# Entries and exits of two block-product feed-forwards, reordered

## What is computed

```python
    x = x + gt2[:, None, :] * ((jax.nn.silu(gate) * up) @ w_down[l])
    return rmsnorm(x, g_final)                 # of first_block
    ...
    h = h + 0.5 * swiglu(rms_norm(h, ffn1_norm[l]), ffn1_w_gate[l], ffn1_w_up[l], ffn1_w_down[l])
    u = rms_norm(h, mix_norm[l])
    z = u @ w_in[l]
    ...
    h = h + merged @ w_out[l]
    h = h + 0.5 * swiglu(rms_norm(h, ffn2_norm[l]), ffn2_w_gate[l], ffn2_w_up[l], ffn2_w_down[l])
    return rms_norm(h, final_norm)
```

## Time and profile before

| | |
|---|---|
| median of the runs | 1738.32 us |
| the profiled execution | 1740.45 us |
| its span, first to last instruction | 1738.6 us |
| mean granted TensorE clock | 0.987 |
| PE matmul busy | 1673.1 us, 96% |
| PE weight load busy | 1424.8 us, 82% |
| DVE busy | 1054.4 us, 61% |
| ACT busy | 735.4 us, 42% |
| POOL busy | 200.5 us, 12% |

### The profile page before, as it was taken

The page is one execution under the profiler, slowest core; times in us unless marked ns, Lnnn a source line. Parts: engine busy times, 40 slices in busy tenths (PEclk is TensorE's granted clock), DMA queues, the critical chain, the costliest instruction groups (busy, mean ns, idle before and its releaser), DMA issues.

```text
span 1738.6 us, 24842 instructions
## 1 busy us (share of the span) xinstructions
PE 1673.1 (96%) x9717; PEld 1424.8 (82%) x9717; DVE 1054.4 (61%) x1586; ACT 735.4 (42%) x1238; POOL 200.5 (12%) x193
## 2 busy tenths in 40 slices
PE   7999999999999978999999989999999899999998
PEld 5777688888888768989899877677887699898997
DVE  4888765433333475776767634766455677586774
ACT  3466544212222444524345322555443554243444
POOL 0120120000000262010010230002001210101102
PEclk9999999999999988999999999999999999999999
DMA  9733145342242537474575136212236474537721
GB/s 331 249 111 123 42 146 175 109 127 76 88 125 69 137 98 186 100 203 119 150 169 146 37 110 113 73 50 70 85 97 169 113 191 138 146 84 202 170 85 49
DMA packets 289159, 219.98 MB, mean 127 GB/s; under 512 B 15995, under 2 KB 275511, under 8 KB 289031
## 3 DMA queue, kind: packets, MB, share of 16 engines
q1 hardware_dynamic: 261056, 181.43, 33.7%
q0 software_dynamic: 27632, 36.89, 11.8%
q10 hardware_dynamic: 360, 0.13, 0.0%
HBM read 215.27 MB, written 6.36 MB: 127 GB/s over the span
## 4 chain that ended last, share of the span: by engine, by line
PE 40%; DVE 10%; ACT 5%; issue 5%; DVEq 0%; ACTq 0%
PE psum L695 9%; PE psum L697 9%; PE psum L696 9%; PE psum L1038 4%; PE psum L1041 3%; PE psum L1040 3%; DVE ring_lo L2179 3%; ACT ring_hi L1626 3%; PE psum L1182 1%; DVE part_raw L2187 1%; PE psum L1147 1%; PE psum L1202 1%; DVE c L2294 1%; DVE g_part L2276 1%; DVE sq L2268 1%
## 5 line engine op out<-in xcount | busy, mean ns | idle before, releaser
L2179 DVE TENSOR_TENSOR ring_lo<-part_raw,ring_hi 128x1024 fp32r<-128x1024 f32 (+1 forms) x270 | 324.7, 1203 | 233.4 <-ACT ring_hi L1626 232.8
L1626 ACT ACTIVATE ring_hi<-part_raw 128x1024 fp32r<-128x1024 f32 (+1 forms) x270 | 277.8, 1035 | 346.9 <-PE psum L697 270.7
L1038 PE MATMUL psum<-hq_hi,ring_hi 128*128 128x256 f32 x1232 | 354.2, 287 | 21.2 <-DVE hq_lo L2370 10.9
L1040 PE MATMUL psum<-hq_lo,ring_hi 128*128 128x256 f32 x1232 | 351.3, 285 | 0.0
L1041 PE MATMUL psum<-hq_hi,ring_lo 128*128 128x256 f32 x1232 | 351.1, 285 | 0.0
L1038 PEld LDWEIGHTS psum<-hq_hi,ring_hi 128*128 128x128 f32 x1232 | 239.2, 194 | 25.7 <-DVE hq_lo L2370 11.5
L1040 PEld LDWEIGHTS psum<-hq_lo,ring_hi 128*128 128x128 f32 x1232 | 239.3, 194 | 0.2
L1041 PEld LDWEIGHTS psum<-hq_hi,ring_lo 128*128 128x128 f32 x1232 | 239.1, 194 | 0.0
L695 PE MATMUL psum<-hid_hi,ring_hi 128*128 128x512 f32 (+1 forms) x536 | 208.5, 389 | 8.7 <-DVE hid_lo L2307 5.2
L697 PE MATMUL psum<-hid_hi,ring_lo 128*128 128x512 f32 (+1 forms) x536 | 207.7, 387 | 0.0
L696 PE MATMUL psum<-hid_lo,ring_hi 128*128 128x512 f32 (+1 forms) x536 | 207.5, 387 | 0.0
(11 more groups left out here) (300 smaller groups left out, 2514.5 us busy)
## 6 DMA issues: line engine op xcount, KB each, us to landing
part_raw<-in_ffn_w_up SPq DMA_DIRECT2D x66, 512.0 KB, 4.9
w_raw<-in_w_in SPq DMA_DIRECT2D x50, 512.0 KB, 3.7
part_raw<-in_w_gate_up SPq DMA_DIRECT2D x44, 512.0 KB, 4.5
part_raw<-in_ffn_w_gate SPq DMA_DIRECT2D x44, 512.0 KB, 5.6
part_raw<-in_ffn_w_down SPq DMA_DIRECT2D x32, 512.0 KB, 4.3
part_raw<-in_ffn_w_gate POOLq DMA_DIRECT2D x22, 512.0 KB, 8.2
part_raw<-in_ffn_w_up POOLq DMA_DIRECT2D x22, 512.0 KB, 10.3
sq<-in_w_ada SPq DMA_DIRECT2D x20, 512.0 KB, 4.8
```

What stands on the lines that cost most here:

```text
L1038: pe.matmul(o, a_hi, b_hi, start=fresh, stop=False, skip_group_check=True)
L1040: pe.matmul(o, a_hi, b_lo, start=False, stop=False, skip_group_check=True)
L1626: act.activation(ring_hi[slot][:, 0:n], pool_raw[s_][b][:, 0:n], ACT.Identity).then_inc(f_high, 1)
L2179: dve.tensor_tensor(ring_lo[slot][:, 0:n], raw_[:, 0:n], ring_hi[slot][:, 0:n].bitcast(F32), ALU.subtract).then_inc(f_ready, 1)
```

## The change

It has these parts.
- The squares of down0 and out2 are no longer added by POOL: `gather` issues, per tile, a DMA that accumulates sq into acc, and waits for its landing before it issues the next. ACT, TensorE and the first and third running copies wait for these landings (`gathered`).
- h is made in three groups per k: A11 and R3; N1 and R2; A12, A22 and N4. N1 and N4 are the negatives of R1 and R4, and signs are turned in the copies and in c12 and c22 to match. DVE makes N1 from x itself, before the second `take_h`, and the item's low part goes between.
- In unit 0 the token sums stand after the second half of B21 and the spreads after T4; the DVE and ACT parts of them move accordingly. B21 waits for all twelve groups.
- In every unit DVE does `first_up` before the item after T1. In the last unit of a round the hidden tiles are formed before the item after B22, and both silus stand after T4.
- The first two slabs of the projection after ffn1 are split before its last down product.
- out2 splits the first three weight items of ffn2 at steps 3, 4 and 6 and the fourth after step 7.
- The near_rows DMAs are issued before `add_weights(1, 0)`.
- In ffn0 the modulation rows are added one unit earlier, and their columns made before the last two hidden tiles enter the first two down products.

```diff
+AHEAD = [3, 4, 6]
...
-        A11, R3, A12, A22, R1, R2, R4 = range(7)
+        A11, R3, N1, R2, A12, A22, N4 = range(7)
...
             def token_sums(name, phase, kinds=1):
 
-                pe.wait_ge(summed, SUM0 + SQUARES[phase] + KD * kinds)
+                if phase in GATHERED:
+                    pe.wait_ge(gathered, 16 * (GATHERED[phase] + KD))
+                else:
+                    pe.wait_ge(summed, SUM0 + SUMMED[phase] + KD * kinds)
...
                 down_part(f, r, order[0], ks[:-2], True)
                 down_part(f, r, order[1], ks[:-2])
+                if between is not None:
+                    between()
                 down_part(f, r, order[0], ks[-2:], True)
                 down_part(f, r, order[1], ks[-2:])
-                if between is not None:
-                    between()
...
-                product(z, "T1", R1, f, u, first=True, ready=None if q0 is None else q0 + 2).then_inc(f_prod, 1)
-                if u == 0:
-                    sums()
+                product(z, "T1", N1, f, u, first=True, ready=None if q0 is None else q0 + 2).then_inc(f_prod, 1)
                 await_item(("T2", f, u))
-                pe.wait_ge(s1_set, m)
+                pe.wait_ge(run_copied, 3 * m - 2)
                 product(y, "T2", R2, f, u).then_inc(f_prod, 1)
                 await_item(("B21", f, u))
+                if u == 0:
+                    pe.wait_ge(q_ready, q0 + 3 * KQ)
...
                 product(x_, "B21", A12, f, u, (1,)).then_inc(f_prod, 1)
                 if u == 0:
+                    sums()
+                await_item(("T4", f, u))
+                pe.wait_ge(run_copied, 3 * m)
+                product(y, "T4", A22, f, u).then_inc(f_prod, 1)
+                if u == 0:
                     spreads()
-                await_item(("T4", f, u))
-                pe.wait_ge(u3_set, m)
-                product(y, "T4", A22, f, u).then_inc(f_prod, 1)
...
                 if u == 0:
-                    act.wait_ge(summed, SUM0 + SQUARES["down0" if f == 1 else "out2"] + KD * (2 if f == 1 else 1))
-                act.activation(s1, psum[:, y, :], ACT.Copy).then_inc(s1_set, 1)
+                    act.wait_ge(gathered, 16 * (KD * f - 1))
+                act.activation(s1, psum[:, y, :], ACT.Copy).then_inc(run_copied, 1)
...
-                wait_summed("down0", i, None, 2)
                 wait_new("down0", i, None, 1)
-                take_h(i, n, "ffn1", gff[:, n:n + 1])
+                take_h(n, "ffn1", gff[:, n:n + 1])
+                if n >= KQ:
+                    parts_high(n % KQ, 1, "ffn1")
+                if i >= 2:
+                    act.wait_ge(gathered, 16 * (i - 1))
                 for m in range(2):
                     act.activation(sq[:, i % 2, m, :], x[:, n, :], ACT.Square,
                                    scale=col_of("g_final", n, None, 1) if m else 1.0).then_inc(squared, 1)
-                parts_high(n, "ffn1")
+                parts_high(n % KQ, 2 if n >= KQ else 0, "ffn1")
...
                 next_h(n, None, 1, col_of("mix_norm_2", n, None, 1))
                 square(n, None)
+                if KQ <= n < KQ + 2:
+                    split_high(S_PROJ2 + n - KQ)
...
+                dve.wait_ge(x_new, new)
+                done(dve.scalar_tensor_tensor(out=h_parts[:, HN1, :], in0=x[:, n, TQ:T], scalar=col, in1=h_parts[:, H21, :],
+                                              op0=ALU.mult, op1=ALU.subtract))
+                dve.scalar_tensor_tensor(out=h_parts[:, H2, :], in0=h_parts[:, HN1, :], scalar=-1.0, in1=h_parts[:, H11, :],
+                                         op0=ALU.mult, op1=ALU.subtract).then_inc(combos_set, 1)
+                if p < KQ - 1:
+                    between()
+                dve.wait_ge(combos_set, gen + 3 * p + 2)
+                dve.wait_ge(h_taken, seen + 2)
+                dve.scalar_tensor_tensor(out=h_parts[:, HN4, :], in0=h_parts[:, H12, :], scalar=-1.0, in1=h_parts[:, H2, :],
+                                         op0=ALU.mult, op1=ALU.subtract).then_inc(combos_set, 1)
+                part_low(1)
+                part_low(2)
+                if p == KQ - 1:
+                    between()
...
+                    if n == KD - 2:
+                        dve.wait_ge(f_prod, max(prod[k] for k in prod if k in ring and k[1] < 2 and in_ring[ring[k]][1] == 3))
+                        split_low(S_PROJ2)
+                        split_low(S_PROJ2 + 1)
...
+            def gather(phase, kinds):
+
+                if phase == "out2":
+                    wait_filled(pool, ("sum", "mix2"))
+                done(pool.memset(acc[:, 0:kinds, :], 0.0))
+                for n in range(KD):
+                    pool.wait_ge(squared, SQUARES[phase] + kinds * (n + 1))
+                    pool.dma_start(acc[:, 0:kinds, :], sq[:, n % 2, 0:kinds, :], accum_op=ALU.add).then_inc(gathered, 16)
+                    pool.wait_ge(gathered, 16 * (GATHERED[phase] + n + 1))
...
             wait_filled(pool, ("mod", GT2 // KD))
+            pool.wait_ge(rpb_copied, 16)
...
-            add_weights(1, 0, *weights1)
-            sums("down0", None, 2)
-
-            pool.wait_ge(rpb_copied, 16)
             for r in range(ROWS):
                 for half in range(2):
...
+                    near_rows_of(r, half)
+            add_weights(1, 0, *weights1)
+            gather("down0", 2)
```

More of the change, by code:

```diff
@@ L1593, in wait_summed @@
             def wait_summed(phase, n, i, kinds=1):
-                v = SUM0 + SQUARES[phase] + kinds * (n - 1)
+                v = SUM0 + SUMMED[phase] + kinds * (n - 1)
                 act.wait_ge(summed, v if i is None else i * 2 * kinds + v)
@@ L1653, in take_h, with parts_high @@
                    .then_inc(h_taken, 1)
-            def parts_high(n, name):
-                act.wait_ge(combos_set, 8 * PAIR_GEN[name] + 2 * (n % KQ) + n // KQ + 1)
-                dst, src = (hq_hi[:, A11:R3 + 1, n % KQ, :], h_parts[:, H11:H3 + 1:2, :]) if n < KQ else \
-                           (hq_hi[:, A12:R4 + 1, n % KQ, :], h_parts[:, H12:H4 + 1, :])
+            def parts_high(p, group, name):
+                act.wait_ge(combos_set, 3 * (KQ * PAIR_GEN[name] + p) + group + 1)
+                dst, src = ((hq_hi[:, A11:R3 + 1, p, :], h_parts[:, H11:H3 + 1:2, :]),
+                            (hq_hi[:, N1:R2 + 1, p, :], h_parts[:, HN1:H2 + 1, :]),
+                            (hq_hi[:, A12:N4 + 1, p, :], h_parts[:, H12:HN4 + 1, :]))[group]
                 act.activation(dst, src, ACT.Identity).then_inc(q_high, 1)
@@ L1862, in _ @@
             for i, n in enumerate(PAIRED):
-                wait_summed("out2", i, None)
                 if i < KD - 1:
                     split_high(S_OUT2 + i + 1)
-                if i >= KQ:
-                    high(FIRST_ITEM[2] + i - KQ)
+                if i in AHEAD:
+                    high(FIRST_ITEM[2] + AHEAD.index(i))
                 wait_new("out2", i, None, 1)
-                take_h(i, n, "ffn2", col_of("ffn2_norm_2", n, None, 1))
+                take_h(n, "ffn2", col_of("ffn2_norm_2", n, None, 1))
+                if n >= KQ:
+                    parts_high(n % KQ, 1, "ffn2")
+                if i >= 2:
+                    act.wait_ge(gathered, 16 * (KD + i - 1))
                 act.activation(sq[:, i % 2, 0, :], x[:, n, :], ACT.Square).then_inc(squared, 1)
-                parts_high(n, "ffn2")
+                parts_high(n % KQ, 2 if n >= KQ else 0, "ffn2")
+            high(FIRST_ITEM[2] + 3)
             def down2(i, n):
@@ L2336, in unit @@
                     second_gate(f, u)
-                low_after("B22", f, u)
-                if last:
                     first_up(f, u)
@@ L2343, in unit @@
                         hidden_low(f, u, h, k)
-                else:
+                low_after("B22", f, u)
+                if not last:
                     first_gate(f, u)
@@ L2562, in _ @@
                 dve.tensor_tensor(x[:, n, :], psum[:, b, :], x[:, n, :], ALU.add).then_inc(x_new, 1)
-                if i >= KQ:
-                    lower(FIRST_ITEM[2] + i - KQ)
-                combos(n, "ffn2")
+                combos(n, "ffn2", NEW_X["out2"] + i + 1, col_of("ffn2_norm_2", n, None, 1),
+                       lambda: lower(FIRST_ITEM[2] + AHEAD.index(i)) if i in AHEAD else None)
+            lower(FIRST_ITEM[2] + 3)
             def cols_ffn2():
@@ L2739, in _ @@
             add_weights(2, 0, *weights2)
-            sums("out2", "mix2")
+            gather("out2", 1)
             for u in range(1, KU):
```

126 lines of the change are left out of this document (60 added, 66 removed).

## The result

The changed kernel takes 1698.74 us, the median of four runs from 1695.91 to 1701.48; the kernel before, 1740.21 (1737.66 to 1744.64). The ratio is 0.9761, 95% interval 0.9743 to 0.9779: faster by 2.4%, 41.5 us between the medians. The profiled execution took 1695.91 us, its span is 1694.0, the mean granted clock 0.994 (before 0.987). Against the profiled execution of before that is 44.5 us. The forecast was 1693.0 with 1684 to 1712: the time lies in it, 5.7 above the forecast, of which 1.9 is the kernel before, whose median is 1740.21 here and was 1738.32 when I added up. But the sum that made the forecast was right in total and wrong in parts.

What follows compares the result with a forecast made beforehand. TensorE, busy for most of the span, was taken as the bound, losing time to late operands and halved clocks at feed-forward borders. Gains of 22 + 7.5 + 11 + 3.5 + 1 = 45 us took 1738.3 to 1693, range 1684 to 1712.

Steps and rivals of the forecast that it cites:

- Entry of ffn1: Down products before ffn1 and its first two units: 27.4 us to be had, less 5.0 at the spreads, taken as 22.
- The gather price: Each 512 KB accumulating DMA of squares before ffn1 takes 5.5 us, with 3.3 and 6.6 kept as bounds.
- the seventh at E+3.8: Seventh gather lands 3.8 us after E, ffn1's first block product; T2 wants s1 at E+5.9, so nothing lost.
- a wait for s1 above 2 us: Sign at ffn1's entry: PE waiting over 2 us for s1 before T2 would show the forecast wrong.
- Exit: Behind ffn1: early weight splits remove the 5.40 us w_lo wait and 2.7 of slow clock; 8.1, taken as 7.5.
- out2 and entry of ffn2: Shorter w_lo and hq_lo waits, slow clock gone, less 1.5 at the spreads, plus the late u2 copy: 11 us.
- Last unit of a round: Feed-forward round ends: first_up and hidden no longer stand behind low(B22+4); waits of 5.2 us shrink, 3.5 gained.
- mod: Modulation rows and columns made earlier: PE's 1.1 us wait before a down product goes, counted as 1.
- the late u2 copy (1.0): Entry of ffn2: first_up before T4's low removes a late u2 copy, 1.0 us, counted within the 11.
- slow gathers: Rival: gathers at 6.6 us make PE wait 5.1 before T2 and 5.8 at the spreads; 1703 us, chance 0.20.
- Fast gathers: Rival: gathers at 3.3 us, spreads waiting about 0.5 and out2's gathers hidden; 1687 us, chance 0.15.
- the vector chain: Rival: splits and parts in out2 and the downs end a microsecond later per step; about 12 us, 1705, chance 0.10.

Runs made afterwards that it cites:

- the variant: Under exit, mod and first_up: that one part alone put into the kernel before; exit 1735.29 us, mod 1737.51, first_up 1732.25.
- The four parts run alone: Each put singly into the kernel before: first_up sooner 1732.25 us, exit splits sooner 1735.29, modulation rows and columns sooner 1737.51, near_rows table loads moved 1729.23.
- mod sooner: Kernel before with only ffn0's modulation rows added one unit earlier and the columns made earlier on TensorE: 1737.51 us, ratio 0.9980.
- root first: Changed kernel with the scales (root, reciprocal, column) ahead of the splits of T1' again in first units, accumulating DMAs kept: 1692.43 us, ratio 0.9740.
- out2 by POOL: Changed kernel with out2's squares added by POOL again, ffn1's entry keeping its accumulating DMAs: 1691.48 us, ratio 0.9723.
- both by POOL: Changed kernel with the squares of both down0 and out2 added by POOL again, all moves kept: 1688.12 us, ratio 0.9700.
- Root first with out2 by POOL: Changed kernel with scales ahead of T1' splits and out2's squares added by POOL, ffn1 keeping its gathers: 1689.29 us, ratio 0.9705.

## Why the prediction was right, and where it was wrong

The sum was 45; the profiled pair gives 44.5, the medians 41.5. By its steps:

- **Entry of ffn1, 22:** 19.6 (16.8 after E, and 2.8 in the down products before it). That the 5.79, 3.14, 1.77 and 5.78 go held. The gather price held: 5.5 forecast, 5.76 in one profile, 5.4 in the other (635.37-592.19 over 8). What failed is "the seventh at E+3.8 ... T2 wants s1 at E+5.9: nothing lost". I had the first down product end 38.2 us before E, as if seven whole ones followed. The first two are completed close together, behind the last hidden tiles: DVE takes the first at 588.31, 33.7 before E. All gathers shift by those 4.5. In the first profile the seventh landed at E+11.0, 7.2 later than forecast: the other 2.7 are the first issue and the gather of 8.15. In the second it landed at E+8.1. PE waited 3.67 and 2.68 for s1. The list of the forecast named it: a wait for s1 above 2 us makes the step wrong. In return the spreads waited 0 and 1.88, not 3.3.
- **Exit, 7.5:** 7.3 to 9.4 by the variant's trace, 5.8 by its medians.
- **out2 and entry of ffn2, 11:** the step that failed. The w_lo waits fell from 9.7 to 4.9 instead of 2.6, and the first units lost 5.6 instead of gaining. The stretch up to E2 gained 15.9, of which the exit is 7.3 to 9.4; that leaves 1 to 3 us for this step. The sentence was "The gathers are 256 KB, about 4.1, under 5.45: hidden. The spreads may wait 1 to 3 for T1'." The first half is true of a gather alone (4.0 us in the median of the eight, from the page's DMA issues) and false of the two that matter: the first stood behind two accumulating DMAs, the last beside five fetches. I had priced them by size, not by what is in flight at their issue, and had carried ffn1's order (T1' ahead of the root) over without looking when add_weights(2, 1) could leave. Taking the gathers out of out2 gave 8.1 back, all of it at the first units. The w_lo waits it did not shorten (5.3), so that these stayed above 2.6 is not shown to be the gathers' doing.
- **Last unit of a round, 3.5:** the two borders of each feed-forward are 0.66 and 1.67 us shorter (64.36 to 63.70, 54.49 to 52.82), with the tail's 0.65 together 5.3. No run has this part alone. The rows of before showed the waits; I had left 0.4 of each standing.
- **mod, 1:** 2.8 in the variant. The wait that I read was 1.1; the rest is the clock behind it, 0.57 over 4 us, which I had not priced here though I had at the other waits.
- **Missing from the sum:** first_up in every unit. Forecast "the late u2 copy (1.0)", for one unit; 0.4 in each of 14 unit-to-unit intervals is 5.7, and with the first units the variant alone made 8.9 us. The row of the u2 copy stood in the trace of before, with its releaser on DVE; only PE's idle times would not show it, since PE lost it in pieces too small for the list of waits.

The 8 to 10 us missing at ffn2 are offset by this term and the smaller ones. That the total came out so near is luck to that extent. The four parts run alone make 8.9 + 5.8 + 3.6 + 11.9 = 30.2 of the 41.5, if their gains add up, which no run tests. The rest belongs to the three groups of h, the order of sums and spreads, the last unit of a round, the early splits in out2 and the gathers together, which were not put singly into the kernel before. Of these the gathers were taken out singly, and they were a net loss: with both entries by POOL and all else kept, the kernel takes 1688.1 instead of 1697.9 to 1698.7.

Of the rivals, slow gathers (6.6 us each) named the right place and mechanism, a new wait at T2 and a longer one at the spreads; the price was not 6.6 everywhere but 4.7 alone and 8 to 11 beside other transfers. Fast gathers did not come. Of the vector chain, the changed kernel shows 1.53 us of waiting for hq_lo at ffn1's entry; with POOL's additions back it was 4.47.

## What to carry to other kernels

A DMA put in place of engine work is priced at its busiest issue, not at its median: list what is in flight when the first and the last of the series leave, since these two gate what stands behind. When an engine's queue is reordered for one stage, check in each other stage that uses the same code when the moved item's input arrives. And read the releasers of a steady unit even where the bottleneck engine shows no wait: 0.4 us a unit was one of the larger terms.

## What was not expected of the hardware

- An accumulating DMA from SBUF to SBUF of 512 KB takes 4.7 us from issue to issue with little beside it (628.31 to 633.02), 8.15 with weight fetches beside it; of 256 KB, 4.0 in the median and 10.7 behind two other accumulating DMAs. The Trainium skill, "DMA: Bandwidth & Descriptors", section on the anatomy of an SWDGE DMA, fits 2.0 us plus bytes over 436 GB/s, by my estimate 3.2 and 2.6 us; these rows are above it even undisturbed.
- Each of five profiles with gathers in ffn1 has one that takes over 8 us (here the one issued at 609.05); the cause is argued from the fetches beside it and wasn't isolated.
- The clock did not follow the length of a wait alone. After 1.97 us of waiting for hq_lo in ffn2 it fell to 0.50 in one profile (mod sooner) and stayed at 1.00 in another (before). After 2.86 us of waiting for s1 (root first) PE went on at 1.00, after 2.33 (out2 by POOL) it fell to 0.56, and after 4.47 (both by POOL) to 0.51. In stretches of PE, out2 by POOL first, root first second:

```profile
630.00:632.00 2.00, 1.25 (x10) 1.00 0.24 49
632.00:634.00 2.00, 2.00 (x13) 0.56 1.09 217
```

```profile
630.00:632.00 2.00, 0.20 (x2) 1.00 0.18 33
632.00:634.00 2.00, 2.00 (x18) 1.00 0.75 152
```

The halved stretch of the first lasts some 4 us (632 to 636), so by my estimate it costs about 2. Root first with out2 by POOL has the same code up to there, waited 2.93 and fell to 0.54, so such a difference can fall between two profiles of the same instructions.
